# Sample attention's value products with the page of values stationary and eight probability columns moving

## What is computed

```python
# q (8 sequences, 8 tokens, 8 heads, 128); k_sel, v_sel: the 256 past positions, lo/v_own: the 8 new ones
ls = jnp.einsum('bqhd,bqhsd->bqhs', q, k_sel) * scale + bias
p = jax.nn.softmax(jnp.concatenate([ls, lo], axis=-1), axis=-1)
return (jnp.einsum('bqhs,bqhsd->bqhd', p[..., :n_s], v_sel)
        + jnp.einsum('bqhk,bkhd->bqhd', p[..., n_s:], v_own))
```

## Time and profile before

| | us |
|---|---|
| median of 3 runs | 1634.09 (1632.97 to 1634.69) |
| the profiled execution | 1633.22 |
| its span, first to last instruction | 1631.5 |
| TensorE busy in the span | 1610.1 (99%) |
| TensorE weight loads busy | 1571.0 (96%) |
| VectorE busy | 1037.3 (64%) |
| ScalarE busy | 627.6 (38%) |
| GpSimd busy | 225.9 (14%) |

### The profile page before, as it was taken

The page is one execution under the profiler, slowest core; times in us unless marked ns, Lnnn a source line. Parts: engine busy times, 40 slices in busy tenths (PEclk is TensorE's granted clock), DMA queues, the critical chain, the costliest instruction groups (busy, mean ns, idle before and its releaser), DMA issues.

```text
span 1631.5 us, 30727 instructions
## 1 busy us (share of the span) xinstructions
PE 1610.1 (99%) x12847; PEld 1571.0 (96%) x12847; DVE 1037.3 (64%) x1651; ACT 627.6 (38%) x794; POOL 225.9 (14%) x354
## 2 busy tenths in 40 slices
PE   7999999999999999999999999999999999999997
PEld 7999989999999999999999999999999999999997
DVE  5675688557444555776656576666666666666666
ACT  6553334323443343733333333333333333333334
POOL 1122322223112121310000000000000101010004
PEclk9999999999999999999999999999999999999999
DMA  8444453446655566445444544445444444444442
GB/s 247 138 143 132 136 162 111 130 137 227 213 168 202 183 201 206 145 142 154 155 149 148 154 145 154 148 146 158 145 155 145 152 152 146 155 145 153 142 156 85
DMA packets 230954, 255.59 MB, mean 157 GB/s; under 512 B 9412, under 2 KB 220934, under 8 KB 230816
## 3 DMA queue, kind: packets, MB, share of 16 engines
q1 hardware_dynamic: 217856, 220.12, 43.8%
q0 software_dynamic: 10272, 32.24, 5.7%
q10 hardware_dynamic: 2688, 1.27, 0.3%
HBM read 242.48 MB, written 12.69 MB: 156 GB/s over the span
## 4 chain that ended last, share of the span: by engine, by line
PE 94%; DVE 4%; DMA 1%; issue 1%; ACT 0%; SPq 0%; DVEq 0%; POOLq 0%; POOL 0%
PE ps_proj L1823 23%; PE ps_proj L1825 22%; PE ps_proj L1824 22%; PE ps_small L1823 6%; PE ps_small L1825 6%; PE ps_small L1824 6%; PE ps_small L1865 2%; DVE w_lo L1209 1%; DVE conv_acc L1252 1%; DMA x_raw<-in_x_sample_dram 0%; PE ps_small L2103 0%; PE ps_proj L1865 0%; PE ps_small L2199 0%; PE ps_small L2217 0%; PE ps_small L1998 0%
## 5 line engine op out<-in xcount | busy, mean ns | idle before, releaser
L1823 PE MATMUL ps_proj<-x_hi,w_hi 128*128 128x320 f32 x2432 | 763.1, 314 | 1.0 <-issue 0.7
L1825 PE MATMUL ps_proj<-x_hi,w_lo 128*128 128x320 f32 x2432 | 751.8, 309 | 0.0
L1824 PE MATMUL ps_proj<-x_lo,w_hi 128*128 128x320 f32 x2432 | 751.5, 309 | 0.0
L840 ACT ACTIVATE w_hi<-w_raw 128x1024 fp32r<-128x1024 f32 x408 | 431.8, 1059 | 718.0 <-PE ps_proj L1825 522.3
L1209 DVE TENSOR_TENSOR w_lo<-w_raw,w_hi 128x1024 fp32r<-128x1024 f32 x408 | 497.6, 1223 | 304.5 <-ACT w_hi L840 304.0
L1823 PEld LDWEIGHTS ps_proj<-x_hi,w_hi 128*128 128x128 f32 x2432 | 457.0, 188 | 11.8 <-issue 8.9
L1824 PEld LDWEIGHTS ps_proj<-x_lo,w_hi 128*128 128x128 f32 x2432 | 457.2, 188 | 0.3
L1825 PEld LDWEIGHTS ps_proj<-x_hi,w_lo 128*128 128x128 f32 x2432 | 456.8, 188 | 0.0
L1823 PE MATMUL ps_small<-hid_hi,w_hi 128*128 128x320 f32 x704 | 217.5, 309 | 0.0
L1825 PE MATMUL ps_small<-hid_hi,w_lo 128*128 128x320 f32 x704 | 217.1, 308 | 0.0
L1824 PE MATMUL ps_small<-hid_lo,w_hi 128*128 128x320 f32 x704 | 217.0, 308 | 0.0
(11 more groups left out here) (351 smaller groups left out, 1154.7 us busy)
## 6 DMA issues: line engine op xcount, KB each, us to landing
w_raw<-in_w_up_dram SPq DMA_DIRECT2D x176, 512.0 KB, 3.5
w_raw<-in_w_in_dram SPq DMA_DIRECT2D x112, 512.0 KB, 4.1
w_raw<-in_w_down_dram SPq DMA_DIRECT2D x88, 512.0 KB, 3.5
w_raw<-in_w_out_dram SPq DMA_DIRECT2D x32, 512.0 KB, 3.7
k_pages<-in_cache_k_dram POOLq DMA_DIRECT2D x32, 256.0 KB, 3.7
v_pages<-in_cache_v_dram POOLq DMA_DIRECT2D x32, 256.0 KB, 4.5
state_s<-in_state_gdn_dram POOLq DMA_DIRECT2D x8, 512.0 KB, 6.0
out_ss_dram<-state_s POOLq DMA_DIRECT2D x8, 512.0 KB, 3.8
```

The costliest lines, as they stand in the source:

```text
L840: act.activation(whi[:, slot], raw[:, slot], ACT.Copy).then_inc(hi_done, 1)
L1823: pe.matmul(o, hi, rhs_hi[:, k0 + kk_, :], start=first and kk_ == 0, stop=False)
L1824: pe.matmul(o, hi, rhs_lo[:, k0 + kk_, :], start=False, stop=False)
L1825: ins = pe.matmul(o, lo, rhs_hi[:, k0 + kk_, :], start=False, stop=last and kk_ == CQ - 1)
```

## The change

`PV` swaps its operands: the page's values of one head, 128 positions by 128, are stationary, and the eight probability columns of that head and sequence move. The output is the transposed one, 128 partitions (the head's dimension) by 8 columns, so the result needs no turn: ScalarE's `PV`, TensorE's `OT` and the tile `o_tok` go out, and ScalarE's `OT` copies from `b3[:, 384:512]` straight to `reg`. The probabilities are no longer padded: one ScalarE copy of 256 columns takes the place of two of 128, and GpSimd clears `q_z` only. The planner's length of `PV` goes from 16 to 24 units. The loads of pages, the scores and the softmax stay.

```diff
-                soft = [..., ("P", "PV", g, 0), ("A", "PV", g, 0), None,
-                        ("P", "OT", g, 0), ("A", "OT", g, 0), None]
+                soft = [..., ("P", "PV", g, 0), ("A", "OT", g, 0), None]
...
-          ("A", "PV", g, 1), ("P", "OT", g, 1), ("A", "OT", g, 1)]
+          ("A", "OT", g, 1)]
...
-                    for i in range(2):
-                        act.activation(diagonal(pz[:, i, :]), b3[:, i * P:i * P + P].rearrange("p (h j t) -> p j h t", h=4, j=4), ACT.Copy)
+                    act.activation(pz[:, :, 0:P], b3[:, 0:2 * P].rearrange("p (i c) -> p i c", i=2), ACT.Copy)
...
-                elif name == "PV":
-                    after(act, "P", "PV", *k)
-                    finish(act.activation(ob[:, :], b3[:, 384:512], ACT.Copy))
                 elif name == "OT":
-                    after(act, "P", "OT", *k)
+                    after(act, "P", "PV", *k)
                     finish(act.activation(reg[g][:, 0:4, SEQ + 32 * q:SEQ + 32 * q + 32],
-                                          b3[:, 0:P].rearrange("p (h s) -> p h s", h=4), ACT.Copy))
+                                          b3[:, 384:512].rearrange("p (h s) -> p h s", h=4), ACT.Copy))
...
                             for h in range(4):
-                                at = P * j + 32 * h
-                                pe.matmul(b3[32 * h:32 * h + 32, 384:512], pz[:, i, at:at + 32], vp[:, j, i, h, :],
-                                          start=j == 0 and i == 0, stop=False, skip_group_check=True)
+                                at = 32 * h + DT * j
+                                pe.matmul(b3[:, 384 + at:384 + at + DT], vp[:, j, i, h, :], pz[:, i, at:at + DT],
+                                          start=j == i == h == 0, stop=False, skip_group_check=True)
                     for h in range(4):
-                        ins = pe.matmul(b3[32 * h:32 * h + 32, 384:512], po[0:NS, 32 * h:32 * h + 32], vt[0:NS, 2, h, :],
+                        ins = pe.matmul(b3[:, 384 + 32 * h:416 + 32 * h], vt[0:NS, 2, h, :], po[0:NS, 32 * h:32 * h + 32],
                                         start=False, stop=True, skip_group_check=True)
...
-                elif name == "OT":
-                    after(pe, "A", "PV", *k)
-                    finish(turn(b3[:, 0:P], ob[:, :], P))
...
-                    pool.memset(qz[:, :], 0.0)
-                    finish(pool.memset(pz[:, :, :], 0.0))
+                    finish(pool.memset(qz[:, :], 0.0))
```

More of the change, by code:

```diff
@@ L262, in att_steps @@
                 soft = [("P", "PT", g, 0), ("A", "PT", g, 0), None,
-                        ("P", "PV", g, 0), ("A", "PV", g, 0), None,
-                        ("P", "OT", g, 0), ("A", "OT", g, 0), None]
+                        ("P", "PV", g, 0), ("A", "OT", g, 0), None]
             s = [x for x in s if x]
```

## The result

The changed kernel takes 1679.08 us (median of 4 runs, 1677.01 to 1679.99) against 1634.11 (4 runs, 1632.97 to 1634.69): ratio 1.0275, 95% interval 1.0258 to 1.0291. It is 45 us slower. The direction is as forecast and the time lies in the range, but not at the forecast of 1659: it is rival 1's, 1678.5. The clock fell inside the new PVs.

The account below looks back on a forecast made before the run. TensorE's queue was taken to bound the kernel, 99% busy; new PVs at 34.3 us less 9.1 for old PVs and 0.3 for OT gave +24.8, so 1634.1 + 24.8 = 1658.9 us. Range: 1654 to 1685 us.

Parts of the forecast that it names:

- the forecast: Whole kernel: the clock stays full through the new PVs, 1658.9 us, within 1655 to 1663; chance 0.63.
- rival 1: Clock falls to half inside the new PVs: 1678.5 us if half way through, 1695 if at once; chance 0.30.
- What bounds the kernel: TensorE, busy 99% of the span with 94% of the chain; sample attention's value products stand in its queue, not hidden.
- What it removes: On TensorE, four old PVs at 2.46 or 2.10 us, 9.12 us in all, and four OT, 0.34 us.
- the sum: On TensorE: 34.3 us for four new PVs of 8.6, less 9.1 for old PVs and 0.3 for OT: +24.8 us.
- 0.113 us a record: In the new PVs, price of each fp32 record loading 128 stationary columns, from six such records: 64 take 7.2 us.
- can't cost less than 0.03: Lower bound on a new PV's record: the 0.03 us of a narrow record with 32 stationary columns in old PV.
- The rule of the Trainium skill: For PV, advises making the short side stationary and packing column tiles, up to four times faster; change an estimated 23 us dearer.
- What costs nothing: ScalarE's and GpSimd's lost work, ScalarE's later OT, later page loads and planner shifts: TensorE waits for none; page cover grows.
- the clock stays: TensorE keeps its full granted clock through the four new PVs, 8.6 us each; chance 0.63.
- 24 records with one moving column: In the kernel's tail, TensorE ran these at a granted clock of 1.00; taken as evidence against the clock falling.
- The reading of the earlier trace as the half level: Near the kernel's start, weight products 0.27 us apart in place of 0.15 were read as 1.2 GHz.

Follow-up runs that it names:

- Experiment 1: The changed kernel with all 128 probability columns moving in every page product in place of eight (values wrong): 1657.51 us against 1633.76, ratio 1.0141.
- experiment 5: The changed kernel with each PV cut into four steps, one per sequence, with weight products between: 1658.51 us against 1633.48, ratio 1.0159.
- experiment 6: The kernel before with only the first 8 of each page's 128 value columns moving (rest of the result wrong): 1630.52 us against 1633.51, ratio 0.9980.
- experiment 9: The changed kernel with column tiles kept, each page stationary in four blocks of 32 columns: 1656.36 us against 1633.62, ratio 1.0133.
- experiment 10: The changed kernel with column tiles kept and PV cut into four pieces with weight products between: 1638.55 us against 1633.79, ratio 1.0029.
- experiment 4: The changed kernel without its page products, only the own positions' products staying (past left out): 1632.74 us against 1633.76, ratio 0.9992.
- experiment 3: The kernel before with only the planner's length of PV changed, 24 in place of 16: 1633.95 us against 1633.76, ratio 1.0001.
- experiment 7: The changed kernel with only 64 of each page's 128 value columns stationary (half the result left out): 1654.94 us against 1633.51, ratio 1.0128.

## Why the prediction came out as it did

- **What bounds the kernel** was right: TensorE's queue, and no wait before or after. Every microsecond of PV came through.
- **What it removes** (9.1 and 0.3 us) wasn't measured by itself. Experiment 1 bears out the difference: +23.75 us where the sum gave +24.8, with the new PV at 8.38 in place of 8.56. My sum was 0.18 too high. The 64 page records took 534.29 - 526.91 = 7.38, which is 0.13 more than the sum had. The own products with their change of tiling took 535.29 - 534.29 = 1.00, where I had 0.9 and 0.4: nothing is marked issue between the last page load and the first own load, so the switch that I priced doesn't show.
- **0.113 us a record** was right (0.114 in experiment 5), also in a run of 64. Its reason was half right. An untiled record goes by its stationary columns (0.060 at 64), but the 0.03 of a record before isn't the narrow load: it is the moving columns, with loads at 0.010 hidden beneath (experiment 6). The bound "can't cost less than 0.03" was therefore wrong, though the sum didn't rest on it.
- **The rule of the Trainium skill** that spoke against the change (TensorEngine Tiling (Array Packing), Performance Considerations) was borne out: the form that it advises took 2.46 us for a PV alone, the untiled one 8.38 at the full clock, 3.4 times as much. That the column tiles are what counts showed in the swapped form too: with them its records took 0.009 us and the kernel, once cut up, 1638.6 us (experiments 9 and 10).
- **What costs nothing** was right. ScalarE's OT waited 14.9 us for PV in the profile after, and no wait of TensorE followed. That the cover of the page loads grows with a longer PV showed from the other side: with a shorter one the page was 1.7 us late (experiment 4).
- **The step that failed** is the choice between the forecast and rival 1: "the clock stays", at 0.63. I weighed 24 records with one moving column at a clock of 1.00 against it. That stretch is 2.1 us long, and a PV four times that. Nor was one execution enough for the stretch itself, as is shown below the list. So the trace of before had no row that could decide, and 0.63 to 0.30 was too sure. That the time lies in the range is owed to the share of rival 1 in it.
- **Rival 1's mechanism** was right, with a sum near the truth by two errors. It had the clock fall half way through and seven weight products afterwards, 4.9 us for each PV. It fell 2.1, 4.8, 3.7 and 5.1 us into the four PVs, and stayed down over everything that followed, score steps and key transposes too: 17.1, 10.2, 13.7 and 10.3 us. Its price is 45.0 - 23.75 = 21 us, 5.3 each. The reading of the earlier trace rows as the half level holds: in the kernel after, 0.27 us from product to product stands beside a granted clock of 0.50.

The stretch of the earlier trace rows stands in every profile, since the change doesn't touch it. In the profile before it ran at the full clock to its end. In the profile after the clock fell in it at 1668.5, 3.2 us after the first of the 24 records (1665.34) and with TensorE busy throughout. Its last group of products, before and after:

```profile
1621.73 1.09 PE L2316 MATMUL ps_proj<-consts,x_normed 128*64 128x128 f32 x8
```

```profile
1668.50 1.97 PE L2308 MATMUL ps_proj<-consts,x_normed 128*64 128x128 f32 x8
```

In experiment 3, the kernel before but for the planner's number, it fell too, 2.7 us after the first of the 24. That it stayed up in the one profile that the prediction had was no argument for the forecast.

That the fall goes by how many columns move is shown by experiment 1 (same loads, same length, 128 columns: no fall). That it also goes by how the light work is bunched is shown by experiment 5 (the same products, spread out: one short fall in place of four long ones). What exactly the chip goes by stays open, and so does why the four falls came 2.1 to 5.1 us into their PVs.

That the gaps of experiment 9 are the supply of instructions is shown only in part: the records are issued without such gaps when there are weight products between them (experiment 10), and an instruction load falls into the run. Which resource is empty, and after how many instructions, wasn't tried, and no transfer is seen during the gap that was looked at.

## What to carry to other kernels

Before you swap the operands of a small product, count columns on both sides. Untiled, a fp32 record cost the load of its stationary columns here however few moved (0.113 us for 128), while four column tiles were loaded side by side beneath their moving columns (0.03). Padding that looks like waste may cost nothing, if the padded side is the one that is hidden. Where TensorE is the bound, price light stretches twice, once at the full clock and once for what the clock takes from everything behind them, and try to break them up with full work. And do not take from one profile that the clock stays through a light stretch: the same stretch may lose it in the next execution.

## What the runs showed of the hardware that I had not expected

- Four column tiles with 32 stationary columns of fp32 and 8 moving: 64 records in 0.63 us and 244 in 2.13, 0.009 to 0.010 us each (experiments 6 and 9). Untiled with 128 stationary columns a record is 0.113 to 0.114 us, with 64 columns 0.060 (experiments 5 and 7).
- At that pace TensorE stands still after 118 to 244 records, for 0.8 to 4.5 us, marked issue (experiment 9).
- At half clock the untiled record takes (504.06 - 499.86) / 19 = 0.22 us (19 records from 499.86 to the first own load of PV(0,0)): the loads slow down with the clock as the products do.
- The same light stretch in the tail ran at the full clock in the profile before and lost it in the profile after and in experiment 3.
- Once down, the clock stayed down through 5 us of key transposes, scores and six weight products (505.9 to 511.4 in the kernel after), and it was back at 548.9 in that kernel, with weight products alone from 545.2 on.
